# Final norm of a two-block network: scaling rows on ScalarE and multiplying by the norm's weights on GpSimd, for six of eight blocks

## What is computed

```python
    y = y_pad[dest] * gates[order][:, None].astype(y_pad.dtype)
    out = jnp.zeros((t, d), xt.dtype).at[token_idx[order]].add(y)
...
        x = x + hierarchical_moe(rms_norm(x, norm_ffn[l]), ...)
    return rms_norm(x, norm_final)

def rms_norm(x, g):
    xf = x.astype(jnp.float32)
    y = xf * lax.rsqrt(jnp.mean(xf * xf, axis=-1, keepdims=True) + EPS)
    return (y * g.astype(jnp.float32)).astype(x.dtype)
```

## Time and profile before

| | us |
|---|---|
| median of 3 runs | 2985.7 (2985.19, 2985.7, 2990.61) |
| the profiled execution's own time | 2990.51 |
| its span, first to last instruction | 2988.8 |
| TensorE, busy | 2765.5 |
| VectorE, busy | 1679.1 |
| ScalarE, busy | 1184.9 |
| GpSimd, busy | 511.9 |

### The profile page before, as it was taken

The page is one execution under the profiler, slowest core; times in us unless marked ns, Lnnn a source line. Parts: engine busy times, 40 slices in busy tenths (PEclk is TensorE's granted clock), DMA queues, the critical chain, the costliest instruction groups (busy, mean ns, idle before and its releaser), DMA issues. The chain is left out here.

```text
span 2988.8 us, 38390 instructions
## 1 busy us (share of the span) xinstructions
PE 2765.5 (93%) x14590; PEld 2416.9 (81%) x14590; DVE 1679.1 (56%) x2113; ACT 1184.9 (40%) x1714; POOL 511.9 (17%) x299
## 2 busy tenths in 40 slices
PE   9989999898899999999998998998999499999993
PEld 7989999798789999988777888666776388888883
DVE  5356655361434334333334832664444699999996
ACT  4342333321321111122334213554433377777774
POOL 3000000002122212200110000002610134444441
PEclk9999999999999999999999999999999699999996
DMA  5342322343121111113313121113302399999996
GB/s 193 101 129 92 97 87 90 119 125 123 67 64 48 43 49 49 47 44 105 141 63 106 43 64 57 37 49 92 106 24 113 139 405 417 416 417 414 414 413 242
DMA packets 244298, 436.92 MB, mean 146 GB/s; under 512 B 21698, under 2 KB 180690, under 8 KB 218594
## 3 DMA queue, kind: packets, MB, share of 16 engines
q1 hardware_dynamic: 234690, 400.88, 37.2%
q0 software_dynamic: 9504, 34.61, 2.9%
HBM read 375.54 MB, written 59.90 MB: 146 GB/s over the span
## 5 line engine op out<-in xcount | busy, mean ns | idle before, releaser
L3456 DVE TENSOR_TENSOR k_w_lo<-k_raw,k_w_hi 128x2048 fp32r<-128x2048 f32 x192 | 433.4, 2289 | 41.0 <-ACT k_w_hi L3392 37.3
L3392 ACT CAST k_w_hi<-k_raw 128x2048 fp32r<-128x2048 f32 x192 | 363.0, 1912 | 67.0 <-PE bank L3312 41.2
L120 PE MATMUL bank<-u_ffn_hi,f_w_hi 128*128 128x342 f32 (+1 forms) x840 | 292.1, 348 | 5.6 <-POOL f_w_lo L1329 5.6
L122 PE MATMUL bank<-u_ffn_hi,f_w_lo 128*128 128x342 f32 (+1 forms) x840 | 293.0, 349 | 0.0
L121 PE MATMUL bank<-u_ffn_lo,f_w_hi 128*128 128x342 f32 (+1 forms) x840 | 292.8, 349 | 0.0
L120 PE MATMUL bank<-u_hi,p_w_hi 128*128 128x342 f32 (+2 forms) x720 | 237.7, 330 | 8.9 <-DVEq L878 6.0
L122 PE MATMUL bank<-u_hi,p_w_lo 128*128 128x342 f32 (+2 forms) x720 | 231.8, 322 | 0.0
L121 PE MATMUL bank<-u_lo,p_w_hi 128*128 128x342 f32 (+2 forms) x720 | 231.7, 322 | 0.0
L3310 PE MATMUL bank<-k_w_hi,k_x_hi 128*128 128x512 f32 x512 | 203.8, 398 | 5.4 <-DVE k_x_lo L3462 5.1
L3312 PE MATMUL bank<-k_w_hi,k_x_lo 128*128 128x512 f32 x512 | 200.5, 392 | 0.0
L3311 PE MATMUL bank<-k_w_lo,k_x_hi 128*128 128x512 f32 x512 | 200.3, 391 | 0.0
(11 more groups left out here) (566 smaller groups left out, 6753.5 us busy)
## 6 DMA issues: line engine op xcount, KB each, us to landing
k_raw<-in_w_e_gate_dram SPq DMA_DIRECT2D x64, 1024.0 KB, 7.1
k_raw<-in_w_e_up_dram SPq DMA_DIRECT2D x64, 1024.0 KB, 7.7
k_raw<-in_w_e_down_dram SPq DMA_DIRECT2D x64, 1024.0 KB, 8.2
d_raw<-in_ffn_w_down_dram SPq DMA_DIRECT2D x44, 512.0 KB, 3.3
p_w<-in_w_in_dram SPq DMA_DIRECT2D x34, 512.0 KB, 4.3
f_raw<-in_ffn_w_gate_dram SPq DMA_DIRECT2D x22, 512.0 KB, 3.7
f_raw<-in_ffn_w_up_dram SPq DMA_DIRECT2D x22, 512.0 KB, 3.7
gate_scratch<-g_out SPq DMA_DIRECT2D x20, 513.0 KB, 6.4
```

The lines of the kernel that those rows point to most:

```text
L120: pe.matmul(out, wh[:, t, :], xh[t][:, c:c + n], start=t == 0, stop=False)
L122: m = pe.matmul(out, wl[:, t, :], xh[t][:, c:c + n], start=False, stop=t == tiles - 1)
L3392: act.copy(wh[:, q, :], raw[:, r, :]).then_inc(hi_made, 1)
L3456: dve.tensor_tensor(wl[:, q, :], raw[:, r, :], wh[:, q, :], ALU.subtract).then_inc(lo_made, 1)
```

## The change

For blocks 3 and 7 (`on_vector`) the last step of the norm stays on VectorE as it was. For the six others it is taken apart in two: ScalarE, right behind the Exp of the block, scales the rows in place by the inverse root, and GpSimd, when that has ended, multiplies them in place by the weights. The counts of finished blocks are kept in two semaphores, and SyncE's store of a block waits for the one that fits. VectorE's order becomes F0 M0 F1 M1 F2 M2 F3 M3 F4 M4 N3 F5 M5 F6 M6 F7 M7 N7. The added instructions are called R (ScalarE's rescale) and T (GpSimd's multiply by weights) below: R0, R1, R2, R4, R5, R6 and T0, T1, T2, T4, T5, T6.

```diff
+        def on_vector(b):
+            return b % 4 == 3
+
+        def done(b):
+            return sum(on_vector(e) == on_vector(b) for e in range(b + 1))
...
             for b in range(NB):
-                sp.wait_ge(normed, b + 1)
+                sp.wait_ge(normed_v if on_vector(b) else normed_p, done(b))
                 sp.dma_start(out[0, b * P:(b + 1) * P, :].rearrange("p (k t) -> p k t", t=P), rows_of(h, b)).then_inc(out_stored, 16)
...
             pool.wait_ge(ended, 2)
+            pool.wait_ge(gain_in, 16)
+            for b in range(NB):
+                if not on_vector(b):
+                    pool.wait_ge(rescaled, done(b))
+                    pool.tensor_tensor(rows_of(h, b), rows_of(h, b), wide(gain[:, :]), ALU.mult).then_inc(normed_p, 1)
...
                 act.activation(ss[:, 2, b:b + 1], ss[:, 1, b:b + 1], ACT.Exp, scale=-0.5).then_inc(squared, 1)
+                if not on_vector(b):
+                    act.wait_ge(squared, 3 * b + 3)
+                    act.mul(rows_of(h, b), rows_of(h, b), ss[:, 2, b:b + 1]).then_inc(rescaled, 1)
...
             def norm(b):
                 dve.wait_ge(squared, 3 * b + 3)
-                if b == 0:
-                    dve.wait_ge(gain_in, 16)
-                dve.scalar_tensor_tensor(rows_of(h, b), rows_of(h, b), ss[:, 2, b:b + 1], wide(gain[:, :]), ALU.mult, ALU.mult).then_inc(normed, 1)
+                dve.wait_ge(gain_in, 16)
+                dve.scalar_tensor_tensor(rows_of(h, b), rows_of(h, b), ss[:, 2, b:b + 1], wide(gain[:, :]), ALU.mult, ALU.mult).then_inc(normed_v, 1)
...
-                if b:
+                if b and on_vector(b - 1):
                     norm(b - 1)
             norm(NB - 1)
```

More of the change, by code:

```diff
@@ L3175, in stage_experts @@
     gathered, stored = (g0, g1), (s0, s1)
-    all_stored, gain_in, first, mixed, squared, normed, out_stored = sems(ctx, nc, "o2", "all_stored gain_in first mixed squared normed out_stored")
+    all_stored, gain_in, first, mixed, squared, rescaled, normed_v, normed_p, out_stored = sems(
+        ctx, nc, "o2", "all_stored gain_in first mixed squared rescaled normed_v normed_p out_stored")
     loaded = sems(ctx, nc, "o2", " ".join(f"in{r}" for r in range(RAW)))
```

## The result

| | before | after |
|---|---|---|
| median of 12 runs, us | 2985.72 (2983.02 to 2990.61) | 2992.74 (2987.74 to 2996.38) |
| ratio after / before | | 1.002, 95% interval 1.0012 to 1.0028 |
| profiled execution, us (span) | 2990.51 (2988.8) | 2994.1 (2992.3) |

What follows compares the result with a forecast made beforehand. VectorE was taken to bound the last 40 us, with stores allowing at most 3.7 us gain. Turns costing 10.0 in place of 5.95 put M7 4.1 later, the end +4.6 to 5.5, taken +5.1: 2990.8 us, range 2985.5 to 2996.0.

Steps and rivals of the forecast that it cites:

- VectorE loses six N's, five of them on the path: VectorE, final part: five N's go from before M7, 5 x 1.19 = 5.95 us; N6 gives nothing.
- R at 1.13 and hidden: ScalarE: each rescale takes 1.13 us, hidden except at block 7, whose square starts some 0.25 us late.
- T at 2.40: GpSimd: each multiply by the weights takes 2.40 us, from the row nearest in size and inputs.
- Rival A: GpSimd's multiply is dearer than 2.40 us, making the end slower by over 0.2%; middle case +8.4 us, 2994.1; chance 0.16.
- T at 2.00: GpSimd: if each multiply takes 2.00 us instead of 2.40, the sum is +2.5 us.
- Turns at 1.08 behind GpSimd's end: VectorE and GpSimd take turns on SBUF; VectorE's held instruction ends 1.08 us behind GpSimd's; 10.0 us in place of 5.95.
- Rival B: VectorE and GpSimd do not get in each other's way; stores bound the end, -3.7 us, 2982.0; chance 0.09.
- Which instructions: VectorE: F2, M2, M4, F6 and M6 take 3.2 to 3.3 us instead of 1.28.
- The end: Behind M7: N7 waits for T6 and ends 5.0 us later; store 7 lands behind store 6, +5.3 us.
- Who gets the turn: T4 alone might wait until after F6, making the end +4.6; the middle of 4.6 and 5.5, +5.1, was taken.
- rival C: VectorE always goes first and the six T run one after another behind the mixing; +5.4 us; chance 0.05.

Runs made afterwards that it cites:

- e10_five: The changed kernel with block 6 also kept on VectorE, five products on GpSimd; final part 35.7 us, +4.1 against before, ratio 1.0013.
- e4_scale_only: Kernel before with ScalarE rescaling six blocks, VectorE multiplying by the weights, GpSimd doing nothing; final part 31.3 us, -0.3 against before, ratio 0.9996.
- e1_beside: Kernel before, whole, with six GpSimd products on idle buffers beside it that nobody waits for; final part 43.3 us, +11.8 against before.
- e0_after: The changed kernel run again unchanged; final part 37.5 us, +6.0 against before, ratio 1.0008.
- e6_four: The changed kernel with VectorE keeping four blocks (1, 3, 5, 7), four products on GpSimd; final part 35.4 us, +3.8 against before, ratio 1.0014.
- e5_free: The changed kernel with GpSimd's product replaced by a fill of an idle buffer; final part 28.1 us, -3.5 against before, ratio 0.9976.
- e8_three: The changed kernel with PSUM operands and products of blocks 0, 2, 4 alone on GpSimd, each released by a later F; 28.0 us, -3.5 against before, ratio 0.998.
- e7_psum: The changed kernel, six products, with F writing to PSUM, M reading it there, N's weights in PSUM; final part 33.4 us, +1.8 against before, ratio 0.9999.
- e3_fill: Kernel before, whole, with six GpSimd fills of an idle buffer beside it; final part 31.6 us, 0.0 against before.
- e2_copy: Kernel before, whole, with six GpSimd copies on idle buffers beside it; final part 35.5 us, +3.9 against before.
- e9_psum_only: PSUM operands alone, all eight norms on VectorE, nothing moved to GpSimd or ScalarE; final part 31.6 us, 0.0 against before, ratio 1.0002.

## Why the prediction was right

The forecast was +5.1 us with the time at 2990.8; the medians lie 7.0 apart, the final part is 6.0 longer, the range held 2992.7.

- *VectorE loses six N's, five of them on the path.* Right. e10_five shows the other side: keeping N6 on VectorE cost nothing.
- *R at 1.13 and hidden.* Right: 1.15, and e4_scale_only lost nothing. Block 7's square started 0.33 us behind M7's end where 0.04 is the least, so 0.29 late; 0.25 was forecast.
- *T at 2.40.* Right within 0.06: T6 took 2.34. Rival A, a dearer multiply or dearer runs of 128, is out. (Its side case, T at 2.00, should read 5.1 - 6 x 0.4 = +2.7, not +2.5.)
- *Turns at 1.08 behind GpSimd's end.* Right, the term that decides. Rival B is out by e1_beside and by the five long instructions.
- *Which instructions.* F2, M2, M4, F6, M6 were forecast, M2, F3, M3, F6, M6 came. T0 asked during F2, not M1, since F1 had not waited 0.58 for its load this time. Three M's and two F's either way, so the sum stood: 3 x 1.97 + 2 x 2.09 in place of 5.95.
- *The end.* N7 stood behind T6 (1.86 us), and store 7 moved behind store 6: SyncE's last two stores after went out 1.1 us apart and landed in 3.2 and 3.6 us. e10_five, without T6, landed at 37.9 us from the first F where 37.9 had been expected.
- *Who gets the turn.* This step failed. At 2103 us in the trace before, GpSimd had waited for one VectorE instruction that was running and had then been passed over by three more, and I gave that half weight for T4. In after and e0_after T4, asked for during M5, got its turn ahead of F6, although F6 waits for nothing in M5 and its row starts 0.08 us before M5's end. The same happened to T2 and T4 in e6_four. No T was passed over in any run, and rival C is out. What was different at 2103 us was not found. The working under *The end* gives 5.3; the 5.5 of this step stands in no sum, and the middle of 4.6 and 5.3 is 5.0. So the step took about 0.3 off the sum, and the full 5.3 was the better value.
- *A missing term.* GpSimd's closing drain, under the last heading, +0.55. From F1 the last store landed 5.4 us later than before, where the full sum had 5.3, and the drain adds its 0.55: the 6.0 that came. The forecast of 5.1 was low by both, and the two did not cancel.

The chances had slower by over 0.2% at 0.37 and same at 0.60. The final part is longer by 0.20%, on that line itself.

## What to carry to other kernels

Before moving elementwise work from VectorE to GpSimd, count the SBUF tensors that the neighbours on VectorE read: where they read two, GpSimd's reads are not parallel work but an insertion, here 2.0 us for each 1.2 taken away. The split paid here once two things were done together for three of the eight blocks: one of VectorE's operands in PSUM, and GpSimd's instruction placed beside the work that then reads one tensor in SBUF (-3.5 us). The PSUM operands alone, with six products placed as they came, were not enough (+1.8 us). And ask first what is next behind the bound: here neither e5_free nor e8_three got more than 3.5 us out of the final part, and the stores had been forecast to allow 3.7.

## What was not expected of the hardware

**GpSimd's closing drain takes 5.5 us.** The closing drains of GpSimd and SyncE, in the trace after and in that of before (line, engine, operation, count, duration in ns, start):

```profile
L3180 POOLq DRAIN  x1: 7859/7859/7859, 2984.3 to 2984.3; - x1
L3180 SPq DRAIN  x1: 7/7/7, 2991.6 to 2991.6; - x1
```

```profile
L3179 POOLq DRAIN  x1: 5456/5456/5456, 2949.7 to 2949.7; - x1
L3179 SPq DRAIN  x1: 7/7/7, 2988.5 to 2988.5; - x1
```

Before, it lay between 2949.7 and 2955.2, under the final part. After, it is issued at T6's start and ends at 2992.1, 5.5 behind T6's end at 2986.6 and half a microsecond behind SyncE's, so all engines wait for it. In e7_psum and e6_four it again ended 5.5 behind T6 and set the end. In e3_fill and e5_free it ended 5.5 behind the last fill, which reads nothing, and in e2_copy 5.5 behind the last copy. So in this kernel an instruction on GpSimd that ends in the last 5.5 us sets the end. At the ends of five earlier stages of the trace before, the same kind of drain ended within 0.1 us of GpSimd's last instruction, so 5.5 us is not the price of a drain as such. GpSimd issues its indirect DMAs in the last stage alone; whether that makes this drain long was not tried.

**The exclusion is one of reads, and one input is enough.** A GpSimd copy with one input held VectorE as a product with two did, and a fill of 1.81 us held nothing. The Trainium skill, "SBUF — State Buffer", section "Who interferes with whom", says both, that GpSimd's reads contend and its mere writes do not; the runs agree, with 0.66 us for each copy, 1.96 for each product and 0.0 for each fill.

**PSUM costs VectorE nothing here.** In e9_psum_only F to PSUM took 1.29, M and N with one operand from two banks at once 1.28, as in SBUF.
